# Second feed-forward's entry in a two-layer fp32 kernel: a weight split moved to GpSimd, one square and two row products moved ahead

## The reference, cut to what matters

```
def rmsnorm(x, g):
    y = x * lax.rsqrt(jnp.mean(x * x, axis=-1, keepdims=True) + EPS)
    return y * g
...
        y = merged @ w_out[l]
        x = x + ga1 * rmsnorm(y, g_post_mix[l])

        h = rmsnorm(x, g_pre_ffn[l]) * (1.0 + sc2) + sh2
        u = jax.nn.relu(h @ w_ff1[l])
        y = (u * u) @ w_ff2[l]
        x = x + ga2 * rmsnorm(y, g_post_ffn[l])
```

## Time and profile before

| | us |
|---|---|
| time, median of 3 runs | 768.65 (767.84 to 768.71) |
| the profiled execution | 767.42 |
| its span | 765.4 |
| TensorE busy (share of the span) | 735.9 (96%) |
| VectorE | 550.0 (72%) |
| ScalarE | 384.1 (50%) |
| GpSimd | 51.3 (7%) |

### The profile page before, as it was taken

The page is one execution under the profiler, slowest core; times in us unless marked ns, Lnnn a source line. Parts: engine busy times, 40 slices in busy tenths (PEclk is TensorE's granted clock), DMA queues, the critical chain, the costliest instruction groups (busy, mean ns, idle before and its releaser), DMA issues.

```text
span 765.4 us, 13235 instructions
## 1 busy us (share of the span) xinstructions
PE 735.9 (96%) x5336; PEld 677.8 (89%) x5336; DVE 550.0 (72%) x940; ACT 384.1 (50%) x546; POOL 51.3 (7%) x72
## 2 busy tenths in 40 slices
PE   5999998999999999998999999999998999999996
PEld 4999986789999999987999999999877999998995
DVE  6797788676787776866669977885986777555554
ACT  7433767655443334446444446565554444444442
POOL 2940000000000000000432000000000000000000
PEclk9999999999999999999999999999999999999999
DMA  8636411357888888661454556544542675545611
GB/s 330 222 119 230 157 60 53 123 208 301 325 340 319 310 323 322 222 221 55 144 191 134 185 221 217 194 173 166 173 176 91 244 260 211 199 165 185 219 56 55
DMA packets 27022, 151.10 MB, mean 197 GB/s; under 512 B 3128, under 2 KB 7836, under 8 KB 9564
## 3 DMA queue, kind: packets, MB, share of 16 engines
q1 hardware_dynamic: 22620, 124.81, 45.2%
q10 hardware_dynamic: 3456, 25.17, 8.2%
q0 software_dynamic: 896, 0.43, 0.3%
HBM read 148.92 MB, written 1.05 MB: 196 GB/s over the span
## 4 chain that ended last, share of the span: by engine, by line
PE 77%; DVE 15%; ACT 4%; issue 2%; DMA 1%; SPq 0%; DVEq 0%; ACTq 0%
PE ps L460 23%; PE ps L461 23%; PE ps L462 23%; DVE ada L1718 3%; DVE w_lo L1628 2%; DMA raw<-wts 1%; PE ps L590 1%; ACT w_hi L1191 1%; PE ps L566 1%; PE ps L1010 1%; DVE extra L1881 1%; DVE rows_ga L1764 1%; ACT rows_ga L1266 0%; PE ps L957 0%; PE ps L533 0%
## 5 line engine op out<-in xcount | busy, mean ns | idle before, releaser
L1628 DVE TENSOR_TENSOR w_lo<-raw,w_hi 128x2048 fp32r<-128x2048 f32 x106 | 239.8, 2269 | 109.2 <-ACT w_hi L1191 109.0
L460 PE MATMUL ps<-h_hi,w_hi 128*128 128x256 f32 (+2 forms) x1000 | 285.7, 286 | 2.3 <-ACT alibi L1451 1.3
L462 PE MATMUL ps<-h_hi,w_lo 128*128 128x256 f32 (+2 forms) x1000 | 282.8, 283 | 0.0
L461 PE MATMUL ps<-h_lo,w_hi 128*128 128x256 f32 (+2 forms) x1000 | 282.8, 283 | 0.0
L1191 ACT CAST w_hi<-raw 128x2048 fp32r<-128x2048 f32 x106 | 198.6, 1886 | 48.7 <-PE ps L462 38.1
L460 PEld LDWEIGHTS ps<-h_hi,w_hi 128*128 128x128 f32 (+2 forms) x1000 | 190.2, 190 | 6.1 <-issue 4.9
L461 PEld LDWEIGHTS ps<-h_lo,w_hi 128*128 128x128 f32 (+2 forms) x1000 | 190.2, 190 | 1.8 <-issue 0.7
L462 PEld LDWEIGHTS ps<-h_hi,w_lo 128*128 128x128 f32 (+2 forms) x1000 | 190.2, 190 | 0.2
L460 PE MATMUL ps<-w_hi,mix_hi 128*128 128x512 f32 x248 | 97.8, 394 | 1.0 <-DVE small L1764 0.8
L461 PE MATMUL ps<-w_lo,mix_hi 128*128 128x512 f32 x248 | 96.8, 390 | 0.0
L462 PE MATMUL ps<-w_hi,mix_lo 128*128 128x512 f32 x248 | 96.5, 389 | 0.0
(11 more groups left out here) (309 smaller groups left out, 963.9 us busy)
## 6 DMA issues: line engine op xcount, KB each, us to landing
raw<-wts SPq DMA_DIRECT2D x113, 1024.0 KB, 4.8
ada<-w_ada ACTq DMA_DIRECT2D x24, 1024.0 KB, 5.1
resid<-x SPq DMA_DIRECT2D x2, 512.0 KB, 4.1
raw<-wts SPq DMA_DIRECT2D x2, 512.0 KB, 6.5
rows_ga<-rows_wide SPq DMA_DIRECT2D x1, 1024.0 KB, 7.0
out<-resid SPq DMA_DIRECT2D x4, 256.0 KB, 2.0
shared<-shared SPq DMA_DIRECT2D x2, 320.0 KB, 6.8
raw<-w_idx SPq DMA_DIRECT2D x1, 544.0 KB, 4.0
```

The lines of the kernel that those rows point to most:

```text
L460: nc.tensor.matmul(o, lh, rh, start=start, stop=False)
L461: nc.tensor.matmul(o, lh, rl, start=False, stop=False)
L462: return nc.tensor.matmul(o, ll, rh, start=False, stop=stop)
L1628: V.tensor_tensor(w_lo[:, s % RING, 0:w], raw[:, n_of[name] % RAW, 0:w], w_hi[:, s % RING, 0:w].bitcast(F32), ALU.subtract).then_inc(w_rea ...
```

## The change

It has three parts.

- The low part of fa1 is made by GpSimd, as its last instruction, when ScalarE has made the high part. It tells so by a semaphore of its own, `fa1_ready`. TensorE waits for that ahead of the first half's tile with fa1, and SP waits for it and for fa0's split ahead of the loop of loads. VectorE's `extra_low("fa1")` is gone.
- On ScalarE the second half's first square comes ahead of the first half's eight pieces. `squares_rows` is cut in two, `first_square_rows` and `last_square_rows`, for that.
- On VectorE the second half's two row products come ahead of the splits of the first half's pieces. `post_rows` is cut in two, `rows_times` and `post_rows`, for that.

```diff
--- before.py
+++ after.py
@@ -281,6 +281,7 @@
         b_z, b_zm, b_abs, b_ln, b_sp, b_c, b_cm, b_att = (sem(n) for n in (
             "b_scores_ps", "b_masked", "b_abs", "b_ln", "b_softplus", "b_sum_ps", "b_sum_masked", "b_att"))
         up_ps, up_a, m_sum, m_hi, m_lo = (sem(n) for n in ("up_ps", "up_used", "merged", "merged_hi", "merged_lo"))
+        fa1_ready = sem("fa1_ready")
         fa_tile, fa_turned, fa_first_hi, fa_first = sem("fa_tile"), sem("fa_turned"), sem("fa_first_hi"), sem("fa_first_ready")
         sqy, y_gain, y_res = sem("squares"), sem("y_gained"), sem("y_residual")
 
@@ -383,7 +384,8 @@
                         load_loop(FF1_LOOP, TURNS_1)
                 elif kind == "s" and s_idx[name] in ff2_tiles:
                     if s_idx[name] == FF2_LOOP:
-                        sp.wait_ge(x_ready, x_no["fa1"])
+                        sp.wait_ge(x_ready, x_no["fa0"])
+                        sp.wait_ge(fa1_ready, 1)
                         load_loop(FF2_LOOP, TURNS)
                 else:
                     load(name)
@@ -452,6 +454,10 @@
                 for b in (0, HD):
                     for to, at in ((b, b + 8), (b + 8, b)):
                         pool.dma_start(partner(r)[to:to + 8, :], src[at:at + 8, :]).then_inc(s_swap[r], 16)
+
+            hi, lo = extras["fa1"]
+            pool.wait_ge(x_hi, x_no["fa1"])
+            nc.gpsimd.tensor_tensor(lo, raw_of("fa1"), hi.bitcast(F32), ALU.subtract).then_inc(fa1_ready, 1)
 
         @block.tensor
         def _(pe):
@@ -1104,7 +1110,7 @@
                 fa = [[a.rearrange("p (k c) -> p k c", k=DC) for a in extras[f"fa{st}"]] for st in range(2)]
                 pe.wait_ge(x_ready, x_no["fa0"])
                 rows_tile(*fa[0], fa_bank(0), 0, rows(0))
-                pe.wait_ge(x_ready, x_no["fa1"])
+                pe.wait_ge(fa1_ready, 1)
                 rows_tile(*fa[1], fa_bank(1), 0, done)
                 keep_warm(6, 4)
                 turn_rows2(1)
@@ -1528,7 +1534,7 @@
             after(s_idx["o20"])
             extra_hi("fa0")
 
-            def squares_rows(m):
+            def first_square_rows(m):
 
                 if m == 0:
                     act.wait_ge(acc_ps, 3)
@@ -1536,6 +1542,9 @@
                     act.wait_ge(pe_tile, s_idx["o23"] + 1)
                 act.wait_ge(sqy, 8 + 3 * m)
                 square(sq_full[:, 0:512], ps[:, 2 * m, :], msum[:, m:m + 1])
+
+            def last_square_rows(m):
+
                 act.wait_ge(y_gain, 2 * m + 1)
                 square(sq_full[:, 512:1024], ps[:, 2 * m + 1, :], part[:, m:m + 1])
                 root(5 + 2 * m, m + 1, m)
@@ -1556,11 +1565,13 @@
                     nc.scalar.activation(h_full[:, k * P:(k + 1) * P], src, ACT.Identity, scale=scl[:, k:k + 1],
                                          bias=modT[:, 24 + k:25 + k]).then_inc(hf_ready, 1)
 
-            squares_rows(0)
+            first_square_rows(0)
+            last_square_rows(0)
             extra_hi("fa1")
             squares_new(0)
+            first_square_rows(1)
             full_rows(0)
-            squares_rows(1)
+            last_square_rows(1)
             squares_new(1)
             full_rows(1)
             after(s_idx["o21"])
@@ -2199,7 +2210,7 @@
                 link(V.reciprocal(rst[:, m:m + 1], sqv[:, m:m + 1]))
                 newton(rst[:, m:m + 1], msum[:, m:m + 1], nwt[:, m:m + 1])
 
-            def post_rows(m):
+            def rows_times(m):
 
                 if m == 0:
                     dve.wait_ge(row_ready, 2)
@@ -2211,6 +2222,9 @@
                         dve.wait_ge(sqy, 9 + 3 * m)
                     V.tensor_tensor(y_norm[:, 2 * m + n, :], ps[:, 2 * m + n, :], rows_ga[:, 0, n * 512:(n + 1) * 512],
                                     ALU.mult).then_inc(y_gain, 1)
+
+            def post_rows(m):
+
                 dve.wait_ge(sqy, 10 + 3 * m)
                 rstd_row(m)
                 dve.wait_ge(y_gain, 2 * m + 2)
@@ -2237,8 +2251,9 @@
             modulation(32, 8, 20)
             modulated("g_pre_ffn", 32)
             dve.wait_ge(x_new, 10)
+            rows_times(0)
             post_rows(0)
-            extra_low("fa1")
+            rows_times(1)
             split_rows2(0)
             post_rows(1)
             split_rows2(1)
```

## The result

| | before | after |
|---|---|---|
| median of the runs, us | 768.67 (767.84 to 768.71) | 777.09 (775.83 to 777.37) |
| the profiled execution | 767.42 | 777.37 |
| its span | 765.4 | 775.4 |
| VectorE busy | 550.0 | 552.0 |
| TensorE busy | 735.9 | 741.1 |

The change makes the kernel slower: ratio 1.0107, 95% interval 1.0091 to 1.0123, so 8.4 us.

The account below looks back on a forecast made before the run. The entry into the second feed-forward was taken as bound by a dependent chain over VectorE, ScalarE and TensorE. Order 0.5, hold 4.0 and clock 1.5 sum to +6.0 us on the median 768.65: 774.6, range 768.8 to 777.3.

Parts of the forecast that it names:

- The order, +0.5: Entry into second feed-forward: reordering makes TensorE's own path the later one, second transposes ready at 579.4 instead of 578.9.
- what was taken from VectorE is thus spent waiting for the last tile: VectorE's freed 2.29 us go into waiting for the output projection's last tile, at 568.48 at the earliest.
- The first rival: GpSimd's hold of VectorE is short or in portions, at most 0.2 us per instruction; 769.2 in all; chance 0.17.
- The hold, +4.0: GpSimd's split keeps VectorE's first-half statistics chain out of SBUF from about 563.7; +4.0 us, bounds 3.2 and 4.9.
- The row named for it: One VectorE instruction near 563.7, sum of squares or the small sum behind it, takes 4 us or more above 0.69.
- the 0.20 us of the earlier trace: Early in the kernel, a 256-element GpSimd scaling held VectorE's subtraction of two SBUF operands: 0.89 us instead of 0.69.
- The lower bound, 0.20 us times 16: Hold from below: 0.20 us for 256 elements of one operand, 16 times as much to read, 3.2 us.
- GpSimd's length: fa1's split on GpSimd takes 4.9 us, 9.5 if a second operand doubles the rate; its length alone costs nothing.
- The clock, +1.5: TensorE idles some 4.5 us before the first transposes, drops to 1.2 GHz; transposes and last tile cost +1.5 us.
- The clock behind it: If TensorE's clock stays low for another such stretch after the last tile, up to 1.7 us more.

Follow-up runs that it names:

- e9: The changed kernel with fa1's split back on VectorE, plus 10 fill records on TensorE between last tile and first half's row tiles; ratio to before 1.0005 (0.9993 to 1.0018).
- e2: The changed kernel with the split of fa1 back on VectorE, so the reordering alone; ratio to before 1.0025 (1.0011 to 1.0038).
- e8: The changed kernel with 6 fill records on TensorE between last tile and row tiles, first set; ratio 1.0074 (1.0047 to 1.0100), profiled with TensorE at 0.65 of its clock.
- e3: The changed kernel with 20 more fill records on TensorE ahead of the first half's transposes; ratio to before 1.0082 (1.0058 to 1.0107).
- e8b: The changed kernel with 6 fill records on TensorE between last tile and first half's row tiles, run again; ratio to before 1.0072 (1.0055 to 1.0088).
- e1: The kernel before with only fa1's low part moved to GpSimd, other work in its old order; ratio to before 1.0056 (1.0036 to 1.0075).
- e7: The changed kernel with GpSimd's split waiting until the first half's normalised rows are written; ratio to before 1.0047 (1.0033 to 1.0062).
- v1: The kernel before with 12 fill records on TensorE ahead of the transposes beginning the second layer's second half; ratio to before 0.9980 (0.9971 to 0.9989).
- e4: The changed kernel with fa1's low part shared, 1024 columns on GpSimd and 1024 on VectorE; ratio to before 1.0061 (1.0038 to 1.0083).

## Why the prediction was right, point by point

Forecast 774.6, range 768.8 to 777.3, slower; measured 777.09. The direction and both mechanisms were right, one term was missed in size. That the result is still in the range, by 0.2 us, is in part luck: the term that was missed lies above its bound (2.29, where 1.7 was allowed), and the hold made room for it, since its own bound was 4.9 and it came to 4.25.

- **The order, +0.5:** 0.37 (e9). The step "what was taken from VectorE is thus spent waiting for the last tile" shows as 3.34 us of idle time ahead of the row products. What the step left out is that the order alone lowers the clock: e2 shows 1.45 us for that. The first rival's "+0.5 and a few tenths, TensorE doesn't idle long enough for the clock" would, by e2, have come out near 1.8, since 2.43 us of idle time were enough there. In the whole change this 1.45 doesn't come on top: the clock is down by then for the wait ahead of it.
- **The hold, +4.0:** 4.25, of bounds 3.2 and 4.9. The row named for it was the one, and the argument from the earlier trace rows carried over from 256 to 2048 elements. That the 0.20 us of the earlier trace rows were a hold was inferred there by comparison with another line; e8's profile confirms it, since GpSimd was through with its scalings when VectorE came to this same subtraction, and it took 0.68 us. The lower bound, 0.20 us times 16, was too low: the hold follows the end of GpSimd's instruction. For the short scaling it doesn't: there the hold was over at 29.62 + 0.20 = 29.82 and GpSimd's row ends at 30.41. The rule of the table is shown for instructions of 1024 and 2048 elements only.
- **GpSimd's length,** 4.9 by its one-operand rows: 4.76. TensorE took fa1 at 583.52, 13.7 us after it was done: its length cost nothing, as said. SP's loads, issued at 570.21, cost nothing either.
- **The clock, +1.5** until the last tile: 1.45 as what e3 and e8b leave, 1.46 by the rows.
- **The clock behind it: this term was mis-sized.** The prediction had 0 in the sum and up to 1.7 in the range, "if the clock stays low for another such stretch". It stayed low for 13.65 us, and TensorE's first row tile took 5.26 us instead of 2.95. By e8b that was worth 2.29 us, on a path that the order had already made the later one. e8b shows that it hangs on the second gap, which the prediction had in its own numbers (1.72 us from the pieces' start, behind 0.7 for the square, so 2.4) and did not read as an idle time.

The measured parts: 0.37 + 4.25 + 1.45 + 2.29 = 8.36, the distance's whole increase. The two halves of the change alone give 4.17 and 1.82, 5.99 together; the other 2.4 come only from both at once. By the sums, 1.5 of it are the slow transposes and tile, which the order puts onto the path on which e1 still had slack, and 0.8 the row tile, which lost 2.29 with two gaps in a row and 1.45 behind one.

That no placement of the split on GpSimd could win here was argued, not tried in full: VectorE saves 2.29 us by it, and is held up to 4.25. It would need over 2 us in which VectorE reads neither two operands of SBUF nor copies within it, and the tried places (e1, e7) have none. The late split in the old order was not run. What else than these two gaps sets how long the low clock lasts stays open.

## What to carry to other kernels

An instruction on GpSimd that reads SBUF isn't beside VectorE but in its place: before moving work there, look at what VectorE runs in the same microseconds, and count as a hold what is left of GpSimd's instruction when VectorE comes to one with two operands in SBUF, or to a copy within it; this matters most where VectorE is on a chain. A new idle time on TensorE can have two prices, itself and the clock behind it; 2.4 us were enough in e2 (and not in e3), and a few matmuls without use in the wait took the second price away, in the entry and, as v1 shows, in a place that nobody had changed. And two edits of which each seems cheap must be added up on the path that both leave, not on the one before.

## What the runs showed of the hardware that I had not expected

- The hold of VectorE lasts until 0.13 to 0.15 us before the end of the GpSimd instruction (2.13 to 4.79 us long; the five profiles of the table, e3's and e8b's), wherever VectorE meets it, and is nothing beside a memset of 1.81 us.
- A held VectorE instruction counts as busy, and the chain of waits calls the time "issue": 4.64 us. Only its length against its own kind gives it away, 4.94 against 0.69.
- Behind a wait, the low clock lasted 3.42 us (e2), 6.83 (e1, e8b, e7) or 13.65 (after); after and e8b differ only in six fill records ahead of the row tiles. In e4 it came back for 3.41 us, in which TensorE worked 0.98, and then fell again for 3.42.
